# Inverse of the 32x32 diagonal blocks on VectorE during the projection, the last two doubling levels on TensorE

## The reference

```
kb = k * beta[..., None]
lmat = jnp.where(strict, jnp.einsum('bnhid,bnhjd->bnhij', kb, k) * decay, 0.0)
tinv = lax.linalg.triangular_solve(eye + lmat, jnp.broadcast_to(eye, lmat.shape),
                                   left_side=True, lower=True, unit_diagonal=True)
u = jnp.einsum('bnhij,bnhje->bnhie', tinv, vb)
w = jnp.einsum('bnhij,bnhjd->bnhid', tinv, kb * jnp.exp(gc)[..., None])
```

## Time and profile before

| | us |
|---|---|
| median of 3 runs (1319.08 to 1321.98) | 1321.41 |
| profiled execution | 1321.02 |
| its span in the trace | 1319.2 |
| projection units, PE | about 38 to 200 |
| levels | 200.6 to 247.0 |
| values, outputs, router | 247 to 355 |
| experts | 355 to about 1312 |

### The profile page before, as it was taken

How to read it: one execution, slowest core, us unless ns; L and a number is a source line. 1 busy time by engine, 2 the same in 40 slices (tenths; PEclk the granted TensorE clock), 3 DMA queues, 4 the chain that set the end, 5 groups by cost and what they waited for, 6 DMA issues and landing times.

```text
span 1319.2 us, 30117 instructions
## 1 busy us (share of the span) xinstructions
PE 1149.6 (87%) x12197; PEld 617.5 (47%) x12198; DVE 266.0 (20%) x708; ACT 241.3 (18%) x560; POOL 239.9 (18%) x471
## 2 busy tenths in 40 slices
PE   4799999997799999996879999976678977699996
PEld 4678869854544444442334444432223422244443
DVE  1044527475211111110101111110001101011113
ACT  2242322123211111110111111110001110111112
POOL 0030103010122222221112222221112211122221
PEclk9899999998599999998989999998879987899998
DMA  9846743157899999999999099999999999999996
GB/s 339 297 137 223 280 123 140 59 223 229 358 399 428 427 390 429 427 428 426 429 424 384 0 393 427 427 427 427 427 427 428 427 427 428 426 427 428 412 419 257
DMA packets 68465, 462.81 MB, mean 351 GB/s; under 512 B 6106, under 2 KB 22555, under 8 KB 43748
## 3 DMA queue, kind: packets, MB, share of 16 engines
q1 hardware_dynamic: 65852, 460.24, 85.1%
q10 hardware_dynamic: 2531, 1.32, 0.4%
HBM read 455.27 MB, written 6.36 MB: 350 GB/s over the span
## 4 chain that ended last, share of the span: by engine, by line
PE 71%; DMA 19%; SPq 4%; issue 2%; DVE 2%; ACT 1%; ACTq 1%; another core or an unknown queue 0%; POOLq 0%; POOL 0%; DVEq 0%
PE psum L596 23%; DMA weights<-in_w_gu 14%; PE psum L623 12%; PE psum L895 6%; PE psum L556 5%; PE psum L574 4%; DMA weights<-in_w_down 4%; SPq L792 2%; PE psum L1139 2%; PE psum L606 2%; PE psum L570 1%; DMA weights<-in_w_ada 1%; PE psum L563 1%; PE psum L850 1%; PE psum L507 1%
## 5 line engine op out<-in xcount | busy, mean ns | idle before, releaser
L596 PE MATMUL psum<-weights,work 128*32 128x512 f32 x3072 | 382.0, 642 | 95.3 <-DMA weights<-in_w_gu 76.8
L596 PEld LDWEIGHTS psum<-weights,work 128*32 128x32 f32 x3072 | 101.9, 115 | 342.7 <-issue 232.2
L2293 POOL TENSOR_SCALAR level_masks_sb<-work 128x128 f32<-128x128 f32 x159 | 124.5, 792 | 638.0 <-PE psum L614 638.0
L2153 DVE TENSOR_TENSOR work<-psum,work 128x256 f32<-128x256 f32 x53 | 22.5, 425 | 839.8 <-PE psum L606 839.8
L623 PE MATMUL psum<-weights,work 128*32 128x256 f32 x3136 | 182.4, 382 | 9.3 <-DMA weights<-in_w_down 9.3
L623 PEld LDWEIGHTS psum<-weights,work 128*32 128x32 f32 x3136 | 96.5, 110 | 78.9 <-DMA weights<-in_w_down 12.9
L1617 ACT COPY work<-psum 128x512 f32<-128x512 f32 x53 | 31.1, 587 | 495.7 <-PE psum L596 495.7
L556 PE MATMUL psum<-work 128*32 128x256 f32 x1296 | 83.4, 391 | 4.2 <-POOL work L2274 4.2
L895 PE MATMUL psum<-work,weights 128*128 128x288 f32 x320 | 83.1, 417 | 3.6 <-ACT work L1410 3.6
L556 PEld LDWEIGHTS psum<-work 128*32 128x32 f32 x1296 | 45.1, 114 | 59.1 <-issue 42.5
L895 PEld LDWEIGHTS psum<-work,weights 128*128 128x128 f32 x320 | 61.2, 194 | 22.1 <-issue 5.7
(11 more groups left out here) (360 smaller groups left out, 1024.7 us busy)
## 6 DMA issues: line engine op xcount, KB each, us to landing
weights<-in_w_gu SPq DMA_DIRECT2D x116, 2048.0 KB, 30.8
weights<-in_w_down SPq DMA_DIRECT2D x58, 2048.0 KB, 32.7
weights<-in_w_ada SPq DMA_DIRECT2D x12, 2048.0 KB, 13.1
work<-in_w_gu SPq DMA_DIRECT2D x12, 2048.0 KB, 29.5
weights<-in_w_in SPq DMA_DIRECT2D x6, 2048.0 KB, 13.5
work<-in_w_down SPq DMA_DIRECT2D x6, 2048.0 KB, 41.4
weights<-in_w_out SPq DMA_DIRECT2D x1, 4096.0 KB, 13.1
weights<-in_state_ssm SPq DMA_DIRECT2D x8, 384.0 KB, 6.3
```

What stands on the lines that cost most here:

```text
L596: last = mm(bank(GB)[SLOTS * n:SLOTS * n + SLOTS, :], xTm[:, k % 2, k // 2, :], gu[:, k % 2, 512 * n:512 * n + 512], start=k == 0, stop=k ...
L2293: ins = g.tensor_scalar(selG[:, c, :], iota_bd if c == 2 else iota, cur[:, 0, c:c + 1], cur[:, 1, c:c + 1], ALU.is_equal, ALU.mult)
```

## The change

The diagonal 32 x 32 blocks of all twelve matrices (4 blocks, 6 heads, 2 chunks = 48) are inverted by forward substitution, one block to a partition, on 48 partitions of DVE. The blocks go to that layout and back through DRAM: ACT issues eight writes in unit 16 (they count up `blk`), and in unit 17 waits for them and issues one read; SP issues one write of the result and, when it has landed, eight reads into T. `solve(j0, j1)` has two DVE instructions for each of 31 columns, and its pieces stand between the other DVE work of units 17 to 21. POOL sets the block buffers and T to zero first. T's transposes into U move to unit 25, `STEPS` keeps levels 5 and 6, two tail transposes move ahead of unit 25, tail banks become five different ones, and DVE's key and gate scalings move to other places among and behind the levels. `qs_sb` is replaced by counts of `rr`, with the same order.

```diff
-        STEPS = [(0, 1)] + [(o, l) for l in range(1, LEVELS) for o in (1, 2)]
+        STEPS = [(0, 1)] + [(o, l) for l in range(FIRST_LEVEL, LEVELS) for o in (1, 2)]
...
+            sp.wait_ge(s["pooled"], 2)
+            sp.wait_ge(s["t0"], 2)
+            sp.dma_start(t_dram.rearrange("c r h i j -> (c r h) i j"), blk_t[0:BLOCKS]).then_inc(s["blk"], 16)
+            sp.wait_ge(s["blk"], 16 * (2 * NBLK + 2))
+            for c in range(2):
+                for r in range(NBLK):
+                    rows = slice(SOLVE * r, SOLVE * r + SOLVE)
+                    sp.dma_start(Tm[c][rows, :, rows], t_dram[c, r].rearrange("h i j -> i h j")).then_inc(s["blk"], 16)
             sp.wait_ge(s["pool_ps"], 2)
...
                 if u == 18:
-                    pe.wait_ge(s["kv_tok"], 2)
-                    pe.wait_ge(s["t0"], 2)
-                    transposed(1, PB, Tm[0], "u0_ps")
...
                 if u == 25:
-                    tail_transposes(1)
                     pe.wait_ge(s["kv_tok"], 6)
+                    pe.wait_ge(s["blk"], 16 * (4 * NBLK + 2))
+                    transposed(1, PB, Tm[0], "u0_ps")
+                    pe.wait_ge(s["tail_rows"], 2)
+                    transposed(2, PA, Tm[1], "u0_ps")
+                    pe.wait_ge(s["u0"], 2)
...
                     evacuate(0, None, Us, "u0_ps", "u0")
+                    act.wait_ge(s["lmat"], 3)
+                    for c in range(2):
+                        for r in range(NBLK):
+                            rows = slice(SOLVE * r, SOLVE * r + SOLVE)
+                            act.dma_start(l_dram[c, r].rearrange("h i j -> i h j"), Lm[c][rows, :, rows]).then_inc(s["blk"], 16)
                 if u == 17:
                     tokens(2, PA)
+                    act.wait_ge(s["blk"], 16 * 2 * NBLK)
+                    act.dma_start(blk_l[0:BLOCKS], l_dram.rearrange("c r h i j -> (c r h) i j")).then_inc(s["blk"], 16)
...
+            def solve(j0, j1):
+
+                for j in range(j0, j1):
+                    n, m = SOLVE - 1 - j, j + 1
+                    tmp = blk_tmp[0:BLOCKS, 0:n * m].rearrange("p (n m) -> p n m", m=m)
+                    below = blk_t[0:BLOCKS, j + 1:, 0:m]
+                    own(tt(tmp, blk_l[0:BLOCKS, j + 1:, j:j + 1].to_broadcast([BLOCKS, n, m]),
+                           blk_t[0:BLOCKS, j:j + 1, 0:m].to_broadcast([BLOCKS, n, m]), ALU.mult))
+                    ins = tt(below, below, tmp, ALU.subtract)
+                    own(ins) if j < SOLVE - 2 else ins.then_inc(s["t0"], 1)
...
-                if u == 16:
-                    t_start(1)
-                    t_start(2)
                 if u == 17:
                     value_scales()
+                    v.wait_ge(s["pooled"], 1)
+                    v.wait_ge(s["blk"], 16 * (2 * NBLK + 1))
+                    solve(0, 3)
                 if u == 18:
                     sample_conv(0)
+                    solve(3, 6)
                 if u == 19:
                     v.wait_ge(s["tn_ps"], 1)
                     tt(Us[0:NS], Us[0:NS], prep_out(0, None), ALU.subtract).then_inc(s["tu_done"], 1)
+                    solve(6, 12)
                 if u == 20:
+                    solve(12, 16)
...
                     qk_decayed(1, PB)
+                    solve(16, 26)
                 if u == 21:
                     qk_decayed(2, PA)
+                    solve(26, SOLVE - 1)
```

More of the change, by code:

```diff
@@ L44 @@
 LEVELS = 7
+FIRST_LEVEL, SOLVE = 5, 32
+NBLK = P // SOLVE
 SLEVELS = 2
@@ L176 @@
  ks_ps kq_ps vm_ps lg_sb sp_new seq_in rb_in kvT_ps kv_tok lmat mix_ps ml modG modG_st modT modT_ps mod_sb norm_ps oT oT_ps o_ms o_ps
- o_root p1 p1_ps poolT pool_ps pooled proj_ps qk_ps qkd qkdT qkdT_ps qs_sb rank_done ring0 ring1
+ o_root p1 p1_ps poolT pool_ps pooled proj_ps qk_ps qkd qkdT qkdT_ps blk rank_done ring0 ring1
  ring2 ring3 root router_ps rr rt_in s_new s_ps s_silu s_taps sc_ps total_ps sel sel_step selg setup_ps setup_sb
@@ L189, in build @@
     gm_dram = nc.dram_tensor("gate_mod_scratch", (SEQS, 4, 4 * P), F32, kind="Internal").ap()
+    l_dram = nc.dram_tensor("l_blocks", (2, NBLK, H, SOLVE, SOLVE), F32, kind="Internal").ap()
+    t_dram = nc.dram_tensor("t_blocks", (2, NBLK, H, SOLVE, SOLVE), F32, kind="Internal").ap()
     ctx = ExitStack()
@@ L207, in build @@
         last_slot = Arena(Mt, SLOT_W)
+        BLOCKS = 2 * NBLK * H
+        blk_l, blk_t = [Arena(Mt, FRONT).at(SOLVE * SOLVE * i, SOLVE, SOLVE) for i in range(2)]
+        blk_tmp = Arena(Mt, FRONT).at(2 * SOLVE * SOLVE, SOLVE * SOLVE // 4)
         def bank(b, n=1):
@@ L516, in finish_level @@
             pe.wait_ge(s["p1"], i + 1)
-            if l > 1:
+            if i == 1:
+                pe.wait_ge(s["tail_rows"], 4)
+            if l > FIRST_LEVEL:
                 pe.wait_ge(s["tt_done"], i - 2)
@@ L1178, in _ @@
             state_products(1, 2)
-            pe.wait_ge(s["qs_sb"], 1)
+            pe.wait_ge(s["rr"], 2)
             outputs(2, 4)
-            pe.wait_ge(s["rr"], 2)
+            pe.wait_ge(s["rr"], 3)
             new_values(0, 0)
@@ L1486, in _ @@
                     tail_row(0)
+                    tail_row(1)
                 if u == 25:
-                    for q in range(1, 5):
+                    evacuate(1, PB, Um[0], "u0_ps", "u0")
+                    evacuate(2, PA, Um[1], "u0_ps", "u0")
+                    for q in range(2, 5):
                         tail_row(q)
@@ L1942, in _ @@
                         masked(j + 2)
-                if i in (3, 5, 7):
-                    decayed_keys((i - 3) // 2)
-                    own(gate_weights((i - 3) // 2))
+                if i == 1:
+                    decayed_keys(0)
+                    decayed_keys(1)
+                else:
+                    decayed_keys(2)
+                    own(gate_weights(1))
                 for j in (i, i + 1):
@@ L1988, in new_states @@
                 ins.then_inc(s["s_new"], 1)
+            own(gate_weights(0))
+            own(gate_weights(2))
             O_0, O_1, O_s = P1[0], Tm[1], Tm[0]
@@ L2008, in _ @@
             v.wait_ge(s["o_ps"], 2)
-            v.wait_ge(s["qs_sb"], 1)
+            v.wait_ge(s["rr"], 2)
             own(tt(O_1, O_1, heads(4, P), ALU.add))
@@ L2196, in _ @@
                 own(g.memset(sq_s[i], 0.0))
+            flat = blk_t[0:BLOCKS].rearrange("p i j -> p (i j)")
+            own(g.memset(flat, 0.0))
+            own(g.memset(flat[:, 0:SOLVE * SOLVE:SOLVE + 1], 1.0))
             g.wait_ge(s["u_sb"], 2)
@@ L2223, in _ @@
                 own(ins) if m == 0 else ins.then_inc(s["pooled"], 1)
+            g.wait_ge(s["diff_ps"], 3)
+            own(g.memset(Tm[0], 0.0))
+            g.memset(Tm[1], 0.0).then_inc(s["pooled"], 1)
             for i, h in enumerate(QK_ORDER):
```

21 lines of the change are left out of this document (8 added, 13 removed).

## The result

| | before | changed |
|---|---|---|
| median, us | 1320.8 (1319.08 to 1321.98, 4 runs) | 1304.25 (1303.17 to 1304.92, 4 runs) |
| profiled execution | 1321.02 | 1304.24 |
| its span | 1319.2 | 1302.3 |

A forecast was written before the change was run, and what follows sets the result against it. The prediction took PE, filled by the levels at 8.05 us a pass, as the bound: levels ending 23 us ahead, less 3.6 us given back before the sample reads, gain 19.3 us, so 1302 us, range 1294 to 1311.

The forecast's parts named there:

- Solve: On DVE: 62 instructions, 22.9 us in all; the queue from X up to the third qk product 33 us.
- X: L blocks landed in their new layout for DVE: claimed at 151 us, bounds 146.4 and 156.6.
- Rival 4: 48-partition solve instructions with a broadcast column run slower than priced; at 2.3 times the price 1328 us; chance 0.06.
- The mark: End of unit 16's transposes, after which ACT issues the L-block writes; the prediction put it at 136.4 us.
- PE behind unit 22: PE waits 5 to 6 us for DVE's third qk product; unit 23 starts at 185.2, 6.0 us late.
- T's trip: T's write and reads through DRAM land in 4.8 us each; back at 205, 1 us before unit 25 ends.
- Mask wait: Before the sample reads PE waits for POOL's masks, behind w_out and the tail stores: 3.6 us given back.
- Passed on in full: A gain before 355 us, at the experts' start, goes on to the end whole: 19.3 us.
- Rival 2: Trips through DRAM are long, each landing 7.4 us: X at 156.6, gain 11, 1310 us; chance 0.17.
- rival 3: Trips through DRAM are short, 2.3 us each: X at 146.4, gain 26, 1295 us; chance 0.11.
- Rival 1: DVE's queue never holds PE, all of the solve hides: gain 27, 1294 us; chance 0.07.
- Rival 5: Nothing gained at the end, the experts' weight stream eats the earlier start; chance 0.04.

The follow-up runs named there:

- again: The changed kernel run once more, unedited; 1304.72 us, ratio 0.9863 to the kernel before.
- spread: Changed kernel with 18 instead of 26 solve columns before the third qk product, the last 7 behind the samples' third convolution; 1307.99 us.
- no_solve: Changed kernel with 30 of the solve's 31 columns left out, all transfers and waits kept; 1292.65 us.
- no_trip: Changed kernel without the read of the L blocks back from DRAM and both waits for it, solving on zeros; 1296.93 us.
- stores_first: Changed kernel with SP issuing the 19 tail-row stores before w_out; 1300.45 us.
- best: Changed kernel with unit 18's convolution ahead of the L-block wait, last solve columns behind units 20, 21 and 22, stores before w_out; 1292.44 us.
- ssm_last: The kernel of best with the eight sample-state loads issued behind w_out; 1312.97 us.
- best_again: The kernel of best run once more, unedited; 1293.74 us, ratio 0.9774 to the kernel before.

## Why the prediction was right, step by step

The forecast was 1302 us (1294 to 1311), the result 1304.25: the mechanism was the predicted one, and the sizes were off in both directions. That the sample reads came within 0.2 us of their forecast place, 229.07 against 229.3, is partly luck, since errors of 1 to 3 us cancel on the way.

- **Solve.** The two 48x192 of a column start 0.39 us apart, as priced, and from X to the end of the third product it took 32.7 us (to its start 31.8) against 33. Rival 4, slow strided columns, fell with these rows.
- **X** was 153.13, not 151. The mark was 0.95 late; the writes landed at about 148.4 and not 146.3, the first of them being issued at 137.80, and ACT issued the read at 148.40. The read took 4.6, as estimated. The Trainium skill, "DMA: Bandwidth & Descriptors", Anatomy of one DMA, gives its formula for DMAs that GpSimd issues, and the prediction carried it over to ACT's and SP's, as an estimate of 2.1 us for 24 KB and 2.5 for 192 KB. Beside the weight stream the trace has 5.0 and 4.6; where little else moved, the result's trip has 1.8 and 2.6. The same page of the Trainium skill, Latency and other measured facts, has HBM access slower at high load. The trace agrees in direction, but no run here tells HBM from the other parts of a landing.
- **PE behind unit 22.** I put the whole delay there, 5 to 6 us. It came in three parts, 1.18 at unit 20's products, 1.86 at the norms and 3.12: DVE's queue already held PE at two earlier places that I had left out (`again` has only the later of the two, 1.32 us). Unit 23 began at 188.08 and not at 185.2: the third product ended at 185.84 and not at 184, which is X 2.1 late less 0.3 of the queue, and 1.0 is the lower clock in L983 and L876. From there to the levels I had 24.7 us, 1.6 of them for the clock and 1.6 for the moved transposes; it took 22.6. The two errors, 2.9 late and 2.1 short, nearly cancel, and the levels start at 210.63 (209.9 forecast). spread and no_solve show the cause: with the queue cut ahead of that product, or without the solve, the levels start 5.6 and 7.7 us sooner than in the changed kernel, 3.8 and 5.9 sooner than in `again`.
- **Levels.** Two passes in 14.16 us (14.2), where before took 46.42 for six: 32.3 us are gone.
- **T's trip** landed after 2.6 and 1.8 us, not 4.8 twice; little else moved then (27 to 197 GB/s between 190 and 200 us). T was back near 199.5 (194.02 + 3.72 + 1.8), 8 us ahead of unit 25's end and not 1.
- **Mask wait.** Forecast 3.6 us through POOL, measured 2.68. w_out left at 207.29, when unit 25 was done, not at 209.3 behind SP's own issues; its landing was 15.2 and not 13.1, so it was there at 222.5, as forecast (222.4), by two errors. POOL started at 225.13, 1.4 earlier than forecast. no_solve and no_trip, where T comes 5 us and more earlier, have a mask wait of 2.68 too: there as here w_out leaves when unit 25 is done, and the levels behind it are of one length. stores_first shows the cause, SP's order, by taking the wait away.

The term that was too small is the masks: four at 0.70 were priced 2.8 us and took 3.80. The chain view of the changed kernel and of spread has them, and the DVE timelines of the two show what ran beside them or ahead of them:

```profile
225.13 3.80 POOL weights L2294 x4
```

```profile
231.52 2.76 POOL weights L2295 x4
```

```profile
224.65 2.35 DVE L1952 TENSOR_TENSOR work<-work 32x768 f32<-32x768 f32 x2
```

```profile
222.64 1.93 DVE L1953 TENSOR_TENSOR work<-work 32x768 f32<-32x768 f32 x2
```

These are the same two gate scalings (L1952 and L1953), which the change moved behind the levels. In the changed kernel they run beside POOL's masks and both are slower; in spread they end 7 us before the masks start, and four masks take 2.76 us. In all four kernels with the 2.68 the second mask ends 0.5 us behind the end of this DVE pair, though POOL's start moves by 0.4 us against it. So about 1 us of the 2.68 goes with DVE's work beside the masks. No run moves the two scalings alone.
- **Passed on in full** is the step that failed, and the largest error left. At the sample reads the gain was 19.5 us against 19.3. Then 2.6 were lost before the experts, of which I had none: 1.6 to the granted clock in the two groups behind the mask wait, the rest further on. I priced the clock behind the first stop and forgot it behind the second. stores_first, with that wait gone, has the two groups at full speed; its whole stretch is 111.7 us (115.2 in the changed kernel), of which the other half is the part that varies without it. From 355 us on the step held.

Rival 2 (long trips, 1310) fell with X and T's landings, rival 3 (short trips, 1295) with X, though T's trip alone was as short as it had it. Rival 1 (all hides, 1294) fell because DVE did hold PE; `best` shows that its time can be had by placing the same work otherwise. Rival 5 fell with the 16.8 us at the end.

Left open is what makes the mark, the read's landing (2.9 to 6.5 us among these traces) and the clock in the later groups vary between executions.

## What to carry to other kernels

Work moved from the bound engine to an idle one is free only if it stands behind whatever the bound engine will ask of that engine next: the same solve cost PE 9 us or 1 to 2 us at the levels, depending on where its pieces stood in DVE's queue and on whether DVE had other work while its operands travelled. When a stage gets shorter, look at which transfers its old length had covered, and at the order in which one queue issues them: two lines moved in SP's order were worth about 4 us (a wait of 2.68 us and 1.6 us of slow products behind it), and the same kind of move one step further cost 19. Two engines that each have time to spare can still slow each other when their work falls together, as POOL's masks and DVE's scalings did. Price the clock behind every stop that is added, not only the first.

## What was not expected of the hardware

- A wait of 2.68 us before the sample reads was followed by slow products in all four kernels that had it (2.74, 2.77, 3.53 and 2.78 us for 1.97); waits of 2.39, 2.18, 1.79 and 0.26 us in the same place were not (1.97 each). spread's wait of 10.03 us and ssm_last's of 16.72 had 3.68 behind them. What decides it is not shown.
- The same kernel differed by 3 us in one later stretch, in the durations of the same products, behind the same wait. `best` and `best_again`, the two groups behind the 2.60 us wait for DVE (over the two groups the mean granted clock is 1.00 in the one and 0.52 in the other):

```profile
238.32 1.60 PE L1121 MATMUL psum<-weights 128*128 128x128 f32 x12 [2.60 <-DVE weights L2007]
239.85 1.97 PE L1114 MATMUL psum<-weights 128*64 128x128 f32 x32
```

```profile
234.07 2.93 PE L1121 MATMUL psum<-weights 128*128 128x128 f32 x12 [2.60 <-DVE weights L2007]
236.93 3.58 PE L1114 MATMUL psum<-weights 128*64 128x128 f32 x32
```

- The issue of the eight state loads by SP took 8.1 to 9.6 us ahead of w_out's transfer and 18.51 right behind it (one trace). What slowed the issue is not shown.
- Four of POOL's masks took 2.76 us with DVE idle and 3.80 beside two DVE scalings, which took 2.35 us for 1.93.
